# Grouping the value products of two attention jobs behind every second job, with a third buffer for the turned softmax weights

## What is computed

```
s = einsum(q, k) * scale                       # per head, 64 wide
p = masked_softmax(s, causal)
o = einsum(p, v)
NSA:  o = g0 * o_cmp + g1 * o_sel + g2 * o_win # three branches, gated
x = layer_norm(ALPHA * x + o @ w_o)
f = (silu(x @ wg) * (x @ wu)) @ wd
x = layer_norm(ALPHA * x + f)
```

## Time and the profile before

| what | value |
|---|---|
| median of 3 runs | 659.43 us (659.05 to 659.87) |
| the profiled execution | 659.21 us, span 657.5 us |
| PE busy | 641.8 us (98%) |
| DVE busy | 399.8 us (61%) |
| ACT busy | 313.1 us (48%) |
| NSA's jobs on PE | about 87 to 139 us of the span |
| MoBA's jobs on PE | about 419.5 to 444.7 us |

### The profile page before, as it was taken

The page is one execution under the profiler, slowest core; times in us unless marked ns, Lnnn a source line. Parts: engine busy times, 40 slices in busy tenths (PEclk is TensorE's granted clock), DMA queues, the critical chain, the costliest instruction groups (busy, mean ns, idle before and its releaser), DMA issues.

```text
span 657.5 us, 8484 instructions
## 1 busy us (share of the span) xinstructions
PE 641.8 (98%) x3265; PEld 512.7 (78%) x3265; DVE 399.8 (61%) x506; ACT 313.1 (48%) x438; POOL 16.3 (2%) x56
## 2 busy tenths in 40 slices
PE   7999999999999999999999999999999999999995
PEld 5887766677888888888867887778788888888874
DVE  4694679868565554444467755786675555544437
ACT  4664578935453444444433645793353344444420
POOL 2000000000000000000000000000100000000001
PEclk8999999999999999999999999999999999999999
DMA  8984311035574555555542654303656555555301
GB/s 299 360 334 183 129 65 65 2 129 191 169 285 187 191 193 191 191 189 179 183 151 94 250 177 173 140 29 125 232 199 253 189 190 191 191 191 191 128 1 64
DMA packets 18574, 113.03 MB, mean 172 GB/s; under 512 B 2800, under 2 KB 3312, under 8 KB 5872
## 3 DMA queue, kind: packets, MB, share of 16 engines
q1 hardware_dynamic: 16384, 102.65, 42.9%
q10 hardware_dynamic: 1008, 5.77, 2.3%
q0 software_dynamic: 1152, 4.19, 1.9%
HBM read 111.56 MB, written 1.05 MB: 171 GB/s over the span
## 4 chain that ended last, share of the span: by engine, by line
PE 86%; DVE 10%; ACT 2%; DMA 1%; issue 1%; DVEq 0%; SPq 0%; ACTq 0%
PE ps L1036 25%; PE ps L1038 24%; PE ps L1037 24%; PE ps L1214 2%; DVE w_lo L685 2%; PE ps L1247 2%; PE ps L1313 2%; PE ps L1229 1%; DVE bn L920 1%; DVE x L934 1%; DVE x L915 1%; PE ps L1155 1%; DMA twice<-x_cols 1%; DVE arena L869 1%; PE ps L1218 1%; ACT w_hi L418 1%
## 5 line engine op out<-in xcount | busy, mean ns | idle before, releaser
L685 DVE TENSOR_TENSOR w_lo<-raw,w_hi 128x2048 fp32r<-128x2048 f32 (+2 forms) x102 | 220.4, 2165 | 102.2 <-ACT w_hi L418 101.8
L1036 PE MATMUL ps<-w_hi,a_hi 128*128 128x512 f32 x592 | 235.8, 398 | 2.3 <-DVE a_lo L685 1.5
L1038 PE MATMUL ps<-w_hi,a_lo 128*128 128x512 f32 x592 | 231.4, 391 | 0.0
L1037 PE MATMUL ps<-w_lo,a_hi 128*128 128x512 f32 x592 | 231.1, 390 | 0.0
L418 ACT ACTIVATE w_hi<-raw 128x2048 fp32r<-128x2048 f32 (+2 forms) x99 | 184.2, 1863 | 96.6 <-PE ps L1038 88.7
L1036 PEld LDWEIGHTS ps<-w_hi,a_hi 128*128 128x128 f32 x592 | 111.6, 188 | 26.7 <-DVE a_lo L685 2.0
L1038 PEld LDWEIGHTS ps<-w_hi,a_lo 128*128 128x128 f32 x592 | 111.4, 188 | 24.0
L1037 PEld LDWEIGHTS ps<-w_lo,a_hi 128*128 128x128 f32 x592 | 111.7, 189 | 21.9
L1036 PE MATMUL ps<-w_hi,h_hi 128*128 128x512 f32 x160 | 62.4, 390 | 0.0
L1038 PE MATMUL ps<-w_hi,h_lo 128*128 128x512 f32 x160 | 62.3, 390 | 0.0
L1037 PE MATMUL ps<-w_lo,h_hi 128*128 128x512 f32 x160 | 62.2, 389 | 0.0
(11 more groups left out here) (150 smaller groups left out, 471.6 us busy)
## 6 DMA issues: line engine op xcount, KB each, us to landing
raw<-stream SPq DMA_DIRECT2D x94, 1024.0 KB, 4.8
arena<-w ACTq DMA_DIRECT2D x4, 1024.0 KB, 13.4
rows<-norms POOLq DMA_DIRECT2D x8, 512.0 KB, 4.6
raw<-stream SPq DMA_DIRECT2D x3, 512.0 KB, 9.1
twice<-x_cols SPq DMA_DIRECT2D x4, 256.0 KB, 7.6
x<-x_rows ACTq DMA_DIRECT2D x1, 1024.0 KB, 4.8
out<-x SPq DMA_DIRECT2D x3, 256.0 KB, 2.1
raw<-stream ACTq DMA_DIRECT2D x2, 256.0 KB, 5.9
```

Source lines behind the costliest of these rows:

```text
L685: return nc.vector.tensor_tensor(dst, a, b, ALU.subtract)
L1036: nc.tensor.matmul(dst, hi, m_hi, start=start, stop=False)
L1037: nc.tensor.matmul(dst, hi, m_lo, start=False, stop=False)
L1038: return nc.tensor.matmul(dst, lo, m_hi, start=False, stop=stop)
```

## The change

The value products leave every even round and are done in pairs in the odd ones. `weighed_after(i)` says which jobs' value products follow T(i): none at an even i, job 0 at i = 1, jobs i-2 and i-1 at an odd i from 3 on. The last job's still follow the loop. Round i becomes:

- PE: S(i+2), T(i), and at odd i: V(i-2), V(i-1), with L(i-1) between them in NSA.
- ACT: C(i), E(i+2), and at odd i H of the jobs weighed in this round that finish an output. H stood ahead of C(i).
- DVE: M(i+2), X(i+1), the quarter, and at odd i O of the same jobs. In NSA this is the place where O stood; in MoBA two O's stand in an odd round and none in an even one, and O(0) moves from round 2 to round 1.

`probsT` has three buffers, the third in a piece of `arena` that nothing used in these stages, and C(i) waits for V(i-3) where it waited for V(i-2).

```diff
-        probsT = arena[:, 4608:6144].rearrange("p (b n) -> p b n", b=2)
+        probsT = [arena[:, 4608:5376], arena[:, 5376:6144], arena[:, 2048:2816]]
...
+        def weighed_after(i):
+
+            return (i - 2, i - 1) if i % 2 == 1 and i >= 3 else (0,) if i == 1 else ()
...
                 for i in range(jobs):
-                    if i >= 2 and job(i - 2)[4]:
-                        outputs_hi(i - 2)
                     if i >= jobs - 2:
                         round_to(u + 3 + i - (jobs - 2))
                     act.wait_ge(pT_done, j0 + i + 1)
-                    if i >= 2:
-                        act.wait_ge(pv_done, j0 + i - 1)
-                    copy(probsT[:, i % 2, :], acc_flat[:, 2048:2816]).then_inc(pT_ready, 1)
+                    if i >= 3:
+                        act.wait_ge(pv_done, j0 + i - 2)
+                    copy(probsT[i % 3], acc_flat[:, 2048:2816]).then_inc(pT_ready, 1)
                     if i + 2 < jobs:
                         exp(i + 2)
-                for i in range(jobs - 2, jobs):
+                    for weighed in weighed_after(i):
+                        if job(weighed)[4]:
+                            outputs_hi(weighed)
+                for i in range(jobs - 1, jobs):
                     if job(i)[4]:
                         outputs_hi(i)
...
-                    if i >= 2 and job(i - 2)[4]:
-                        outputs_lo(i - 2)
+                    for weighed in weighed_after(i):
+                        if job(weighed)[4]:
+                            outputs_lo(weighed)
                     if i >= jobs - 2:
                         rest_to(u + 3 + i - (jobs - 2))
-                for i in range(jobs - 2, jobs):
+                for i in range(jobs - 1, jobs):
...
-                    if i >= 1:
-                        weigh_values(job, j0, i - 1, a0)
+                    for weighed in weighed_after(i):
+                        weigh_values(job, j0, weighed, a0)
                 weigh_values(job, j0, jobs - 1, a0)
```

More of the change, by code:

```diff
@@ L1237, in weigh_values @@
                 t, _, cols, first, last_one = job(i)
-                b = i % 2
                 pe.wait_ge(pT_ready, j0 + i + 1)
@@ L1247, in weigh_values @@
                     nc.tensor.matmul(dst[HD * h:HD * (h + 1)], values[:, 0, cols[h]:cols[h] + HD],
-                                     probsT[:, b, S * h:S * (h + 1)], start=j0 > 0, stop=False)
+                                     probsT[i % 3][:, S * h:S * (h + 1)], start=j0 > 0, stop=False)
                 for h in range(2):
                     last = nc.tensor.matmul(dst[HD * h:HD * (h + 1), P:S], values[:, 1, cols[h]:cols[h] + HD],
-                                            probsT[:, b, 512 + P * h:512 + P * (h + 1)], start=False, stop=last_one)
+                                            probsT[i % 3][:, 512 + P * h:512 + P * (h + 1)], start=False, stop=last_one)
                 last.then_inc(pv_done, 1)
```

## The result

| | median us | runs |
|---|---|---|
| before | 659.26 | 659.05 to 659.87 |
| after | 668.33 | 668.25 to 669.49 |

The ratio is 1.014, with a 95% interval of 1.0128 to 1.0152: 9.1 us slower, for 668.0 predicted. The profiled execution took 668.4 us, with a span of 666.7 for 657.5 before.

A forecast was written before the change was run, and what follows sets the result against it. The prediction took PE to bound the kernel, with DVE close behind. NSA's +5.6 and MoBA's +3.2 made +8.8 us on the profiled 659.21, giving 668.0 us, range 665.5 to 669.8.

The forecast's parts named there:

- PE and DVE in balance before: NSA before: from even S to odd T, DVE's way and PE's own work both take 3.73 us.
- NSA, +5.6: NSA: PE idles 0.80 us at each odd T, pairs take 6.77 us for 5.77; 5.6 us more in sum.
- T to S as T to V: PE in NSA: the step from T to S costs 0.75 us, like T to V.
- H and O hidden in NSA, with 0.3 to spare: NSA: the later H and O finish 4.0 us after odd T, before S(i+3) is complete at 4.3 us.
- MoBA, +3.2: MoBA: 2.25 us later up to T(7) and 1.0 at the end, 3.2 us more in sum.
- T(5) to R +0.75: MoBA after T(5): two value products stand where one stood, 0.75 us more.
- round 6 -1.0: MoBA's round 6: V(5) leaves its place between T and R, 1.65 us becomes 0.66, 1.0 us less.
- the end +1.0: MoBA's end: V(7) waits for H(5) and O(5), output weights' fourth tile for O(7); together 1.0 us more.
- MoBA's queue would be hidden: Rival, chance 0.1: NSA as forecast, but DVE's low parts in MoBA find their inputs ready; 665.6 us.
- Only the array's changes: Rival, chance 0.05: only PE's array mode changes cost time, DVE is no later than PE; 659.8 us, no change.
- Faster: Rival, chance 0.02: V to L and T to S cost nothing, even rounds save entry and exit; -3.8, 655.4 us.
- Worse than said: Rival, chance 0.08: slowed ACT uses up NSA's 0.3 us and adds some 0.3 a pair; 669.8 us and over.

The follow-up runs named there:

- e7: New kernel with one of two row reductions left out on DVE for NSA's even jobs from 4 on, which changes the output: 665.76 us.
- e8: Kernel before the change with one of two row reductions left out on DVE for NSA's even jobs from 4 on: 658.56 us.
- e6: New kernel with the two value products of each NSA pair in the other order, V(i-1) ahead of V(i-2): 666.76 us.
- e4: Kernel before the change, plus the third buffer and the high part moved behind the exponentials on ACT, PE and DVE as before: 667.81 us.
- e10: New kernel with MoBA's low parts one round later on DVE, behind row maxima and scaling of the even round: 666.48 us.
- e1: Kernel before the change with only NSA's 16 jobs grouped, MoBA's as before: 664.56 us.
- e2: Kernel before the change with only MoBA's 8 jobs grouped, NSA's as before: 662.51 us.
- e9: New kernel with DVE's scaling of the next odd job put ahead of the row maxima in NSA's even rounds from 4 on: 668.20 us.

## Why the prediction was right

- **PE and DVE in balance before.** Right. 3.73 us on both sides was the reading that carried all; e7 and e8 bear it out from either side.
- **NSA, +5.6.** +5.62 in the profile. (R of before starts at 128.55 in the timeline; the 128.62 read from the chain is 0.07 late, which doesn't move the sum.) The pair was put at 6.77 and is 6.77: S to odd T 3.74, then 0.80, 0.80, 0.63, 0.80. T(3) was unmoved: 10.15 us after S(2) after, 10.12 before. The price of an exit into the whole array, taken from a weight product, held for L, 0.63 to the next V.
- **T to S as T to V.** Right, within 0.01: 0.74 (115.38 to 116.12).
- **H and O hidden in NSA, with 0.3 to spare.** Right: 0.26 of idle remained, and e6, which took 0.35 off the pair, used it up. "If that cover is gone, the excess lengthens the pair" was not tried on the new kernel. e4 shows it on the ungrouped one, where the late low part makes the pair 6.42 for 5.77.
- **MoBA, +3.2.** +2.86 up to the output weights and 0.3 at their fourth tile. Its terms, said and measured: T(3) +1.2, +1.16; T(3) to T(5) 6.5 to 6.65, 6.51, which is +1.24 where the sum took +1.3; T(5) to R +0.75, +0.70; round 6 -1.0, -1.05; the end +1.0, 1.1.
- **The rivals.** That MoBA's queue would be hidden fell by the 1.54 us that T(3) waits; e10, where the low parts are moved, comes to 666.5 where that rival had 665.6; the 0.65 us lost at the output weights, which the rival doesn't have, is most of the difference. Only the array's changes: fell by e1 and e2. Faster: by everything. Worse than said: not in the median; its mechanism, ACT using up the 0.3, wasn't seen in the new kernel.

The stages and the end make +8.8 us, which is the forecast's sum. The medians are 9.1 apart, and the execution that was taken as the start lay 0.05 under the median of before, so the time came near by the terms of the sum and not by luck. The largest error of a term is 0.1.

What stays open: why the two attentions apart give 8.7 in the medians and together 9.1, which is within the runs' spread; how much of MoBA's +2.9 is the place of the low parts on DVE and how much the late high part that they wait for; and whether a high part between copy and exponentials would have made the grouped kernel better.

## What to carry to other kernels

Before moving an engine's work behind a wait, ask what that work covers: lay out the timeline by starts and compare the other engines' way between two points with the bound engine's own work between the same two points. A value product of 0.8 us "on the critical path" was also what hid 3.73 us on DVE, and taking it from there cost its whole length in every pair. A long idle entry in a list of waits need not be on the way (1.4 us of the low part), and exchanging the two steps that a wait names need not take it away (in e9 the odd T waits 0.85 as before and the pair is 0.33 longer).

## What was not expected

TensorE's clock can fall behind the wait that the change opened in MoBA. In e9's profiled execution PE stood for 1.54 us ahead of T(3) at 434.39. From 435 to 436 the granted clock was 0.50 of full, the lower of its two levels, 1.2 GHz, and from 436 to 438.3 it was 0.54. The views of busy time by stretch, e9 first, then the new kernel 0.71 us later, where its jobs stand at the same place (T(3) at 435.11):

```profile
430.00:434.00 4.00, 2.67 (x22) 1.39 (x18) 2.60 (x10) 3.28 (x15) 0.00 (x0) 1.00 0.01 6
434.00:436.00 2.00, 1.61 (x8) 1.19 (x10) 1.96 (x8) 1.25 (x6) 0.00 (x0) 0.68 0.00 0
435.00:436.00 1.00, 1.00 (x6) 0.57 (x6) 0.96 (x5) 0.28 (x1) 0.00 (x0) 0.50 0.00 0
436.00:438.30 2.30, 2.30 (x18) 1.41 (x14) 0.40 (x2) 2.30 (x10) 0.00 (x0) 0.54 0.00 0
```

```profile
430.71:434.71 4.00, 2.67 (x22) 1.39 (x18) 2.60 (x10) 3.28 (x15) 0.00 (x0) 1.00 0.01 4
434.71:436.71 2.00, 1.60 (x16) 1.30 (x18) 1.97 (x8) 1.66 (x6) 0.00 (x0) 1.00 0.00 0
436.71:439.01 2.30, 2.30 (x26) 1.64 (x22) 0.66 (x3) 2.28 (x11) 0.00 (x0) 1.00 0.00 0
```

The first stretch is the same in both to 0.01 us, and so is the way from S(2) to T(3), 9.5 us; one fell and one kept its clock. What decides it no run here shows. With the fall MoBA took 28.88 us to the output weights instead of 28.02: 0.9 us. e2 and e6 had such a fall at the same place in their profiled executions too (MoBA 28.83 and 28.82), and e4 had one behind another wait, 1.66 us for the low part ahead of the output weights: 0.57 of full from 454 to 458. All three were the slowest of their four (663.62 for a median of 662.51, 667.86 for 666.76, 669.75 for 667.81), and e9's was too, by less (668.57 for 668.20). The new kernel's own slowest run, 669.49 at a mean clock of 0.992 for 0.994 in the others, may be one; there is no trace of it.
